# Retention scores from 32-row slices of the keys and the queries, without masked copies of the queries

## The reference

```python
def step(s, qkv):
    qc, kc, vc = qkv
    inner = jnp.einsum('bhqd,bhkd->bhqk', qc, kc) * decay_in
    y = (jnp.einsum('bhqk,bhkv->bhqv', inner, vc)
         + jnp.einsum('bhqd,bhdv->bhqv', qc * decay_q, s))
    s = s * decay_chunk + jnp.einsum('bhkd,bhkv->bhdv', kc * decay_k, vc)
    return s, y
...
yl_f, _ = retention_scan(ql, kl, vl, log_gamma[0], sc_f)
yl_b, _ = retention_scan(flip(ql), flip(kl), flip(vl), log_gamma[1], sc_b)
ret_l = retention_out(yl_f + flip(yl_b), zl[4], ret_gn_w)
```

## Time and profile before

| | us |
|---|---|
| median of 3 runs (3000.02 to 3004.13) | 3000.42 |
| span of the profiled execution | 3001.2 |
| its time outside the span | none listed |
| PE busy | 2756.9 (92%) |
| DVE busy | 906.9 (30%) |
| ACT busy | 589.1 (20%) |
| retention of layer 0, first score to last value product | 287.9 to 337.7 |
| retention of layer 1, first score to last value product | 1813.0 to 1855.5 |

### The profile page before, as it was taken

How to read it: one execution, slowest core, us unless ns; L and a number is a source line. 1 busy time by engine, 2 the same in 40 slices (tenths; PEclk the granted TensorE clock), 3 DMA queues, 4 the chain that set the end, 5 groups by cost and what they waited for, 6 DMA issues and landing times.

```text
span 3001.2 us, 41007 instructions
## 1 busy us (share of the span) xinstructions
PE 2756.9 (92%) x16044; PEld 1999.4 (67%) x16044; DVE 906.9 (30%) x1560; ACT 589.1 (20%) x1124; POOL 422.4 (14%) x640
## 2 busy tenths in 40 slices
PE   6888899986999999999997898998699999999996
PEld 2454377544788788788786463764487887887885
DVE  2463655161111111111113576633211111111115
ACT  3312244030111111111111422422011111111111
POOL 0000000004222122122120000000421221221220
PEclk9998999997999999999998999999899999999998
DMA  7563000013778778888876320001488777777765
GB/s 293 215 249 135 1 1 1 28 43 131 295 304 321 302 302 330 315 308 312 325 300 231 114 74 14 1 15 56 177 314 308 289 298 296 300 297 294 295 264 199
DMA packets 97139, 626.39 MB, mean 209 GB/s; under 512 B 32048, under 2 KB 36912, under 8 KB 69936
## 3 DMA queue, kind: packets, MB, share of 16 engines
q1 hardware_dynamic: 53968, 562.34, 48.9%
q0 software_dynamic: 43104, 63.14, 5.7%
HBM read 628.99 MB, written 83.39 MB: 237 GB/s over the span
## 4 chain that ended last, share of the span: by engine, by line
PE 81%; DVE 8%; ACT 4%; DMA 4%; issue 2%; another core or an unknown queue 2%; SPq 0%; DVEq 0%; POOLq 0%; ACTq 0%
PE psum L801 33%; PE psum L816 17%; PE psum L498 15%; PE psum L681 3%; PE psum L657 3%; DVE arena L1498 2%; DMA arena<-in_mod_w 2%; ACT arena L1102 2%; PE psum L491 2%; PE psum L671 2%; PE psum L597 2%; DMA arena<-y 1%; DVE arena L1188 1%; PE psum L571 1%
## 5 line engine op out<-in xcount | busy, mean ns | idle before, releaser
L801 PEld LDWEIGHTS psum<-arena 128*128 128x128 f32 x8832 | 1010.4, 192 | 67.3 <-issue 67.3
L801 PE MATMUL psum<-arena 128*128 128x128 f32 x8832 | 1011.3, 275 | 1.7 <-DVE arena L1492 1.7
L498 PE MATMUL psum<-arena 128*128 128x512 f32 (+1 forms) x1360 | 525.6, 545 | 46.6 <-ACT arena L1090 15.8
L816 PE MATMUL psum<-arena 128*128 128x512 f32 x1104 | 506.7, 602 | 20.8 <-DVE arena L1498 11.1
L498 PEld LDWEIGHTS psum<-arena 128*128 128x128 f32 x1360 | 266.3, 199 | 299.3 <-issue 254.4
L816 PEld LDWEIGHTS psum<-arena 128*128 128x128 f32 x1104 | 198.4, 189 | 247.5 <-issue 247.5
L1498 DVE TENSOR_TENSOR arena<-psum,arena 128x256 f32<-128x256 f32 x138 | 58.5, 424 | 936.6 <-ACT arena L1102 936.6
L1587 POOL DMA_INDIRECT y<-arena,SIX x144 | 148.5, 1031 | 1166.1 <-DVE arena L1506 1126.4
L1506 DVE TENSOR_SCALAR arena<-psum,SIX 128x512 f32<-128x512 f32 x138 | 103.6, 751 | 440.1 <-PE psum L816 440.1
L1102 ACT ACTIVATE arena<-psum 128x256 f32<-128x256 f32 x138 | 52.9, 384 | 889.7 <-PE psum L801 889.7
L1110 ACT ACTIVATE arena<-psum,SIX 128x512 f32<-128x512 f32 x138 | 94.8, 687 | 451.5 <-PE psum L816 451.5
(11 more groups left out here) (194 smaller groups left out, 1708.6 us busy)
## 6 DMA issues: line engine op xcount, KB each, us to landing
arena<-in_experts SPq DMA_DIRECT2D x138, 3072.0 KB, 10.6
arena<-in_mod_w SPq DMA_DIRECT2D x48, 1024.0 KB, 7.3
arena<-y SPq DMA_DIRECT2D x20, 1536.0 KB, 16.8
arena<-in_wblk SPq DMA_DIRECT2D x22, 1024.0 KB, 4.8
arena<-in_shared SPq DMA_DIRECT2D x2, 3072.0 KB, 9.9
hrows<-arena SPq DMA_DIRECT2D x10, 512.0 KB
arena<-in_xT SPq DMA_DIRECT2D x1, 3072.0 KB, 16.4
y<-arena,SIX POOLq DMA_INDIRECT x144, 9.6
```

Source lines behind the costliest of these rows:

```text
L498: last = mm(job(l, key, n, parts), a, b, start=i == 0, stop=i == len(pairs) - 1)
L801: last = mm(psum[:, b, o * P:(o + 1) * P], WB[:, b, k * 512 + o * P:k * 512 + (o + 1) * P], HT[:, b, k, :], start=k == 0, stop=k == KC - 1)
L816: last = mm(psum[:, 3 + j, :], AT[:, b, f, :], WB[:, b, 4096 + f * D + j * 512:4096 + f * D + (j + 1) * 512], start=f == 0, stop=f == 1)
```

## The change

The scores of head h take only the 32 partitions of that head, of the keys and of the queries, instead of all 128 of the keys against a masked copy. The masks, the buffer `QM` and PE's wait for them go. The score tile, its bank, the decay product, the value products and every order by hand stay as they are. `headmask` stays in the constants, unused.

```diff
-        QM = H[:, 4:8, :]
...
                 pe.wait_ge(sem(f"rope{l}"), 2)
-                pe.wait_ge(sem(f"q_masked{l}"), HEADS_R)
...
-                    mm(psum[:, u % 4, 0:n], RK[:, kt * P:(kt + 1) * P], QM[:, h, a:a + n],
+                    mm(psum[:, u % 4, 0:n], RK[h * DK_R:(h + 1) * DK_R, kt * P:(kt + 1) * P],
+                       RQ[h * DK_R:(h + 1) * DK_R, a:a + n],
                        start=True, stop=True).then_inc(sem(f"ret_s{l}"), 1)
...
                 ready(dve, l, ("kr", 1))
-                w = SEG[pl.sq[-1]][0] + SEG[pl.sq[-1]][1]
-                for s in pl.sq:
-                    evacuated(dve, l, ("rq", s))
-                for h in range(HEADS_R):
-                    V.tensor_scalar(QM[:, h, 0:w], RQ[:, 0:w], c("headmask")[:, h:h + 1], None, ALU.mult
-                                    ).then_inc(sem(f"q_masked{l}"), 1)
                 rope("kr", CAT[0:ROPE, 7, 0:LAT], ROPE)
```

## The result

The changed kernel takes 3017.24 us (median of 4 runs, 3015.06 to 3021.88) against 3000.99 us before (median of 4, 3000.02 to 3004.13). The ratio is 1.0051, 95% interval 1.0037 to 1.0065. The forecast was 2992.4 us, with a range from 2988.5 to 3001.5: wrong, on the wrong side.

The account below looks back on a forecast made before the run. PE was taken to bound the run, with DVE late in the retention's first half. Gains of 5.7 us per layer, 11.4, less 3.4 for the clock, gave 8.0 us off 3000.42: 2992.4 us, range 2988.5 to 3001.5.

Parts of the forecast that it names:

- Where the change acts: Whole run: the change can touch only the two retention stages; what they gain reaches the end.
- The masks at 0: Before the scores: removing masks and their wait gains 0, hidden under PE's and ScalarE's work; 2.2 us if exposed.
- The overlap: Score pairs: two heads' scores overlap like value products, 1.01 us for 1.91 (512 queries), 0.58 for 1.06 (256).
- no overlap: Rival for the score pairs: row slices take turns; gain 0, 3000.4 us; chance 0.13.
- half an overlap: Rival for the score pairs: three pass times in place of four; 2996.7 us; chance 0.08.
- exposed weight loads: Rival for the score passes: each pays 0.19 us for its load, without overlap; 3011.4 us; chance 0.08.
- the sum at an unchanged clock: Both retention stages: 5.7 us gained in each layer, 11.4 us together, before any toll of the clock.
- The DVE-paced half: First half of layer 0's stage: DVE's queue moves 1.4 to 1.6 us ahead; pair 7's value products gain 1.6 us.
- The formula: Stage entry at low clock: overlapped scores take 1.71 us, then 2.18 us to the third decay product, 1.5 us earlier.
- The clock: Both stages: longer PE waits for DVE add two low stretches, 1.7 us each, 3.4 us lost; bounds 0 to 6.8.
- The clock stays low: Rival: longer waits keep the clock at 0.50 into the PE-paced half; some 5 us lost, 3006 us; chance 0.05.
- PE-paced half: Second half of layer 0's stage: three 512-query and three 256-query score pairs on PE's path gain 4.1 us.

Follow-up runs that it names:

- s12: Changed kernel with the four masked copies still made and waited for but not read by the scores; 2996.6 us, ratio 1.0088 to the kernel before.
- s2: Changed kernel with DVE's norms all before unit 0 and 12 full matmuls right before the first score; 2973.42 us.
- s7: Changed kernel with full matmuls on constants before the loop and in the loop's waits; 2955.49 us against 2974.31, ratio 0.9941.
- s8: Kernel before (masks, full scores) with full matmuls on constants before the loop and fewer in its waits; 2963.63 us, ratio 0.9963.
- s5: Changed kernel with 12 full matmuls before the first score, DVE's norms left where they were; 3013.27 us beside 2974.31.
- s9: Changed kernel with full matmuls on constants only before the loop, none in its waits; 2990.89 us beside 2973.4.
- s1: Changed kernel with DVE's reciprocals and scalings all done before unit 0 instead of between the decay products; 2990.01 us.
- s3: Kernel before, masks kept, with scores over the pair's 64 rows instead of 128, so without overlap; 3026.82 us against 2967.82.
- s10: Changed kernel with full matmuls on constants only in the loop's waits, none before it; 2966.03 us beside 2973.4.
- s4: Every second pair of scores on 32-row slices, the others on masked copies over 128 rows; 2965.89 us beside 2967.82.
- s11: The changed kernel again, unaltered, on another chip; 2992.44 us, ratio 1.007 to the kernel before.
- s6: Kernel before with 64-row scores, DVE's norms before unit 0 and 12 full matmuls before the first score; total time not given.

## Why the prediction was wrong, point by point

**Where the change acts.** Right in the main: the two stages grew by 16.9 us, the span by 15.4. The prediction let nothing else move; the stretches outside shifted by +1.2, +1.5 and -4.2 us in the two profiled executions.

**The masks at 0.** The traces bear it out at the entry: the first decay product follows the last norm after 2.7 us with the masks (s12) and without. The timed comparison is too coarse to confirm it for the whole program.

**The overlap.** Right, in kind and in size. The summed pair was 2.02 us; s2 and s7 show 2.07 us at 1.00, and the changed kernel has the four loads of a pair at the front. The rivals of no overlap, of half an overlap and of exposed weight loads are out. With the clock held, the change was worth 9.1 us in the stages (s7 against s8, with s8's 0.6 us in it); the sum at an unchanged clock was 11.4. The Trainium skill ("TensorE: Matmul & The Clock Gate", "Measured speedup vs the span model") gives 3.07 times for four row slices with N=512; here two slices take 1.06 us (309.43 to 310.49 in s2) where two full matmuls took 1.91, 1.8 times.

**The DVE-paced half.** The formula was right at the entry, where the clock is low in both kernels. The fourth decay product came at 298.21 in the changed kernel, 9.13 us after the first score (289.08); before, it came 10.71 us after it (287.91 to 298.62): 1.58 us gained, 1.5 summed. The value products of pair 7 were to gain 1.6 us as well. They came at 324.11, 35.03 us after the first score instead of 32.37: 2.7 us lost, because every later score and value product ran at the low clock. The prediction names a reciprocal of 3.34 us for each four products; the second and the fourth in layer 0 take 1.74 us. The wait of 3.7 us that it had worked out did come where the clock was high (3.77 us in s5 and s9), and not in the changed kernel (2.17 us).

**The clock.** This is the step that failed. It counted low stretches by waits, two before and four after, of 3.3 to 3.4 us each, and put 3.4 us for the two more. So it took it for granted that a low stretch ends by itself, the one at the entry above all. In the kernel before the full scores end it. Of its low stretch at 300, the clock is at 1.00 again from 304 on with nothing but scores and value products on PE, and the low stretch at the entry ends at 293.0, when PE has run nothing but full scores since 287.91:

```profile
292.50:293.00 0.50, 0.50 (x2) 0.18 (x1) 0.00 (x0) 0.00 (x0) 0.00 (x0) 0.50 0.00 0
293.00:293.50 0.50, 0.50 (x2) 0.19 (x1) 0.20 (x1) 0.00 (x0) 0.00 (x0) 0.99 0.00 0
```

In the changed kernel the clock was low at the entry and nothing in the stage raised it: in place of 3.4 us for low stretches the runs show one low stretch as long as the stage, and a stage of layer 0 that is 9.5 us longer instead of 4 to 6 us shorter. s1 (no wait after the first, PE busy for 40 us, 0.50) against s2 (the same loop entered at 1.00, which stays) shows that; s3 shows that the rows do it and not the overlap; s5 and s9 show that after a wait of 3.77 us the clock falls and stays down to the end of the stage; s10 shows that full matmuls bring it back.

**The rival that came true.** "The clock stays low" was among the rivals, with a chance of 0.05 and 3006 us. What it describes is what happened, a low clock through the PE-paced half. The cause that it names, "the longer waits", is not: the waits were no longer than before (2.17 and 1.51 us), the clock was low from the entry on, and s3 stays low with no wait at all. Its price was too small as well. A 512-query pair in the PE-paced half took 3.91 us (3.8 had been put), so three of them lost 3.0 us against 2.92. Pairs with 256-query scores lost as well: 1.0 us each where the value products still had 512 columns (335.85 to 338.91, then to 341.97), 0.57 us for each of the next two, 0.8 us at the end. With the 2.7 us from the DVE-paced half that makes 2.7 + 3.0 + 2.0 + 1.1 + 0.8 = 9.6 us in layer 0, and the stage grew by 9.5. The rival's 5 us come without a sum. Its own 0.9 us a pair, over the some 12 PE-paced pairs of the two layers that the prediction counts elsewhere, would have been over 10 us. The prediction gave it so little weight because no row of before had a lasting low clock under a busy PE; but none had 32-row matmuls either, and the chance should have been that of an unknown, not that of an exception.

**What stays open.** How the chip weighs rows and columns was not measured. Seen were only these cases: 64 rows in all scores did not raise the clock (s3), full rows in every second pair did (s4). Whether the masks are worth 0 or 2 us a layer stays within the noise of the times of s11 and s12, though not in their traces at the entry. The totals of s1 to s6, s9 and s10 are single runs and carry no interval; for these only the clock and the distances within the stage are relied on.

## What to carry to other kernels

Rows that are only multiplied by zeros look idle, but here it was the scores that took them in that raised the clock. Before cutting such rows, look at whether the stretch enters at the low clock and what in it will still raise it. A sum made at one clock level must be made again at the other; here the same edit costs about 16 us or, with the clock held, gains 6.5 to 8. Where PE waits anyway, full matmuls on constants into an unused bank held the clock at a cost of 0.2 us in layer 0 (s7); started at the low clock, they delayed the value products by 4 us (s10).

## What the runs showed of the hardware

- A stage of 32-row scores (two overlapping) and full value products, PE busy for 40 us, did not leave 0.50; the same stage entered at 1.00 stayed there. 64-row scores without overlap behaved alike (60 us busy at 0.50 in s3; 1.00 held in s6).
- Two float32 matmuls on neighbouring 32-row slices, into different banks, run at the same time, much as two on column halves do: 1.06 us for both at 1.00 with 512 columns (column halves 1.01), 2.01 us at 0.50.
- 59 us were lost in s3 (one run against one, 53 of them in the two stages) by taking in 64 instead of 128 rows, with not one instruction more or less (41007 in both). The rows left out were multiplied by zeros only.
- After a wait of 3.77 us the clock fell from 1.00 to 0.50 and 32-row scores did not bring it back (s5, s9, both layers); after one of 2.31 us in the kernel before it fell and full scores brought it back.
